# The inverse of each 64-step chunk in an RWKV scan, kept in compressed blocks

## The reference, cut to what matters

```python
def wkv_scan(state0, r, dec, k, v, kk, a, reverse):
    emit = r is not None

    def step(S, inp):
        d_t, k_t, v_t, kk_t, a_t = inp[:5]
        sa = jnp.einsum("bhvk,bhk->bhv", S, -kk_t)
        S = (S * d_t[:, :, None, :] + sa[..., None] * (kk_t * a_t)[:, :, None, :]
             + v_t[..., None] * k_t[:, :, None, :])
        out = jnp.einsum("bhvk,bhk->bhv", S, inp[5]) if emit else None
        return S, out
```

## Time and profile before

| | us |
|---|---|
| median of 3 runs | 2809.04 (2806.54 to 2811.82) |
| profiled execution, its span | 2808.7 |
| scan stage, its first to its last instruction, about | 1073 to 1758 |
| PE busy / DVE / ACT / POOL in the whole span | 2512.4 / 1519.4 / 1099.4 / 735.1 |

### The profile page before, as it was taken

One profiled execution on the slowest core, in us unless ns is written; L12 is line 12 of the kernel. 1 busy time (PEld: TensorE's weight loads), 2 busy tenths in 40 slices (PEclk: granted clock), 3 DMA queues, 4 the chain that ended last, 5 costly groups with the idle time before them and its releaser, 6 DMA issues. The chain is left out here.

```text
span 2808.7 us, 66348 instructions
## 1 busy us (share of the span) xinstructions
PE 2512.4 (89%) x28704; PEld 1935.4 (69%) x28704; DVE 1519.4 (54%) x2491; ACT 1099.4 (39%) x1771; POOL 735.1 (26%) x422
## 2 busy tenths in 40 slices
PE   7998899999889995888888887889999999898997
PEld 5776577777667784777777776768788655475666
DVE  4744589863652213556666663344542466525975
ACT  4633321152453433455545543334422344323133
POOL 2422301422212225555545551100000000032132
PEclk9999999999899996999999999989999999998998
DMA  4224344434335531111111100633522100044431
GB/s 159 83 68 135 128 135 124 122 105 162 116 125 183 201 122 59 43 43 55 38 54 54 32 15 26 240 129 103 159 79 86 57 0 1 11 173 139 137 109 68
DMA packets 90286, 272.63 MB, mean 97 GB/s; under 512 B 13584, under 2 KB 14608, under 8 KB 89872
## 3 DMA queue, kind: packets, MB, share of 16 engines
q1 hardware_dynamic: 73104, 229.25, 25.6%
q10 hardware_dynamic: 16896, 39.16, 4.0%
HBM read 203.01 MB, written 36.70 MB: 85 GB/s over the span
## 5 line engine op out<-in xcount | busy, mean ns | idle before, releaser
L375 PE MATMUL ps<-h_parts_conv,w_parts_one 128*128 128x512 f32 x3168 | 579.8, 343 | 16.9 <-DVE h_parts_conv L361 13.7
L375 PEld LDWEIGHTS ps<-h_parts_conv,w_parts_one 128*128 128x128 f32 x3168 | 492.4, 190 | 107.5 <-issue 24.1
L375 PE MATMUL ps<-scratch_scan 64*64 64x64 f32 (+1 forms) x16704 | 383.1, 234 | 96.2 <-issue 56.1
L375 PEld LDWEIGHTS ps<-scratch_scan 64*64 64x64 f32 x16704 | 345.9, 137 | 139.5 <-issue 105.8
L372 ACT ACTIVATE scratch_scan<-ps 128x384 f32<-128x384 f32 x560 | 238.4, 495 | 331.7 <-PE ps L375 180.3
L443 POOL TENSOR_TENSOR w_parts_one<-ring,w_parts_one 128x1024 fp32r<-128x1024 f32 x83 | 208.2, 2509 | 581.4 <-ACT w_parts_one L372 581.3
L375 PE MATMUL ps<-h_parts_attn,w_parts_rwkv_out 128*128 128x512 f32 (+1 forms) x1536 | 329.2, 373 | 4.6 <-DVE h_parts_attn L369 4.6
L375 PEld LDWEIGHTS ps<-h_parts_attn,w_parts_rwkv_out 128*128 128x128 f32 x1536 | 263.2, 189 | 64.0 <-issue 9.4
L443 POOL TENSOR_TENSOR w_parts_rwkv_out<-ring,w_parts_rwkv_out 128x1024 fp32r<-128x1024 f32 x31 | 74.6, 2409 | 812.5 <-ACT w_parts_rwkv_out L372 812.5
L369 DVE SCALAR_TENSOR_TENSOR scratch_conv<-scratch_conv,vec 128x512 f32<-128x512 f32 (+1 forms) x408 | 252.6, 691 | 0.2
L372 ACT ACTIVATE w_parts_rwkv_out<-ring 128x1024 fp32r<-128x1024 f32 x104 | 109.5, 1056 | 344.0 <-PE ps L375 325.8
(11 more groups left out here) (219 smaller groups left out, 3263.6 us busy)
## 6 DMA issues: line engine op xcount, KB each, us to landing
ring<-in_weights SPq DMA_DIRECT2D x311, 512.0 KB, 3.7
rwkv_spill<-scratch_conv ACTq DMA_DIRECT2D x64, 384.0 KB, 2.3
stream<-rwkv_spill SPq DMA_DIRECT2D x64, 384.0 KB, 3.6
scratch_conv<-scratch_conv SPq DMA_DIRECT2D x120, 103.1 KB, 2.2
scratch_conv<-scratch_conv SPq DMA_DIRECT2D x120, 67.4 KB, 2.0
x_spill<-stream ACTq DMA_DIRECT2D x16, 384.0 KB, 2.5
kept_gate<-scratch_attn ACTq DMA_DIRECT2D x64, 64.0 KB, 2.6
y_spill<-scratch_scan SPq DMA_DIRECT2D x8, 384.0 KB, 2.5
```

What stands on the lines that cost most here:

```text
L375: return nc.tensor.matmul(o, l, r, start=start, stop=stop)
```

## The change

- The inverse is stored compressed. For blocks of b, each row keeps only the b columns of its own block. A level's result is written so that those columns stand repeated over the 64 columns of the chunk (`own`, `half_of`). The full block diagonal form is needed for the transposed P alone, and comes from a mask at the eviction (`own_block`).
- T(n) is 12 matmuls in place of 24. The stationary operand is 64 rows x 128 columns (N of both heads of a pair of chunks), the moving one has 2b columns. Q(n) is 12 as well, with a stationary operand of 128 rows x 64 columns and 2b moving columns. ACT evicts T in two instructions of 64 partitions each, into a tile (`TZ`) of which the other halves stay zero.
- The first doubling becomes a level too (n = 0, b = 1): `first_t` with 6 matmuls of 128 x 128 weights and 4 moving columns, `first_q` with 2, two tiny evictions (`first_t_copy`), and one DVE instruction. `first_inverse`, `p_start` and `p_diagonal` are gone. Levels are now numbered 0 to 5.
- The update is one DVE instruction of 128 x 384 for a level in place of two. Before it ACT writes the part that stays (`other_half`): ten instructions of 128 x 384 for a unit.
- The transposed P of levels 1, 2 and 3 is evicted by DVE with a mask (`turned_inverse`, two instructions each). That of levels 4 and 5 (blocks of 16 and 32) is evicted by ACT, one instruction for each block column with a scale for each row (`turned_blocks`, 8 and 4 instructions). P6, the whole inverse, is evicted by ACT as before.
- The transposed K moves from DVE to ACT.
- POOL masks N in one instruction of 128 x 768 for a level in place of two of 128 x 384. There are six levels for a unit in place of five.

The core of the diff:

```diff
-            def inv_t(w, lv):
...
-                for j in range(HALFC):
-                    for h in range(2):
-                        for par in range(2):
-                            last = mm(bank3(par)[HS[h], j, :], NT[(NLV * w + lv) % 2][HS[par], 2 * j + h, :], PQ[w % 2][HS[par], 2 * j + h, :])
+            def inv_t(w, n):
+                pe.wait_ge(n_masked, masked_at(w, n))
+                inverse_ready(pe, w, n)
+                b = inner(n)
+                for j in range(HALFC):
+                    for par in range(2):
+                        last = mm(PS[:, par * 512 + 2 * b * j:par * 512 + 2 * b * (j + 1)].rearrange("p (x b) -> p x b", x=2),
+                                  NT[n % 2][HS[par], 2 * j:2 * j + 2, :].rearrange("p h t -> p (h t)"), PQ[(n - 1) % 2][HS[par], 2 * j:2 * j + 2, 0:b])
...
+            def inv_q(w, n):
+                pe.wait_ge(t_copied, 2 * product_at(w, n))
+                for e in range(2):
+                    pe.wait_ge(*read_at(f"P{n}", w, e))
+                b = inner(n)
+                t = TZ[:, :, 0:NSTEP * b].rearrange("p x (y j b) -> p y j x b", y=2, b=b)
+                for j in range(HALFC):
+                    for par in range(2):
+                        last = mm(PS[HS[par], 2 * b * j:2 * b * (j + 1)].rearrange("p (x b) -> p x b", x=2), PT[w % 2][:, 2 * j + par, :], t[:, par, j])
+                last.then_inc(q_done, 1)
...
+            def first_t(w):
+                pe.wait_ge(n_masked, masked_at(w, 0))
+                room_for(pe, "T0", w, 0)
+                first = fill_bank("T0", w, 0) * 512
+                o = PS[:, first:first + 2 * NSTEP].rearrange("p (x j y) -> p j y x", x=2, y=2)
+                ones = C("own_half").rearrange("p (y x) -> p y x", y=2)
+                for j in range(HALFC):
+                    last = mm(o[:, j, :, :], NT[0][:, 2 * j:2 * j + 2, :].rearrange("p h t -> p (h t)"), ones)
...
+            def inverse_update(w, n):
...
+                    v.wait_ge(q_done, product_at(w, n))
+                    inverse_ready(v, w, n)
+                    q = PS[:, 0:NSTEP * b].rearrange("p (g b) -> p g b", b=b)
+                    if n < NLV - 1:
+                        v.wait_ge(halved, halved_at(w, n))
+                        vtt(into, into, own(n, q), ALU.add).then_inc(added, 1)
...
+            def turned_inverse(w, n):
+                for e in range(2):
+                    v.wait_ge(*done_at(f"P{n}", w, e))
+                    vtt(blocks(n, PT[w % 2][:, half(e), :]), blocks(n, bank3(fill_bank(f"P{n}", w, e))), own_block(n)).then_inc(*read_inc(f"P{n}", w, e))
...
+            def other_half(w, n):
...
+                    inverse_ready(a, w, n)
+                    before = own(n, PQ[(n - 1) % 2][:, :, 0:inner(n)])
+                    if n < NLV - 1:
+                        act(half_of(n, d), before, ACT.Copy, scale=keep).then_inc(halved, 1)
+                    act(into, before, ACT.Copy, scale=by).then_inc(halved, 1)
...
+            def turned_blocks(w, n):
+                b, first = inner(n), 2 * CH + (8, 12)[n - 4]
+                for e in range(2):
+                    a.wait_ge(*done_at(f"P{n}", w, e))
+                    into, o = PT[w % 2][:, half(e), :], bank3(fill_bank(f"P{n}", w, e))
+                    for k in range(CH // b):
+                        last = act(into[:, :, k * b:k * b + b], o[:, :, k * b:k * b + b], ACT.Copy, scale=C("own_block", first + k, 1))
+                    last.then_inc(*read_inc(f"P{n}", w, e))
```

More of the change, by code:

```diff
@@ L1793, in two_blocks @@
         NT = [take(NSTEP, CH) for _ in range(2)]
-        T1, MT, NE = (take(NSTEP, CH) for _ in range(3))
+        MT, NE = (take(NSTEP, CH) for _ in range(2))
+        TZ, TZ0 = take(2, HALFC * CH), take(2, NSTEP)
         BONV = [take(TT) for _ in range(3)]
@@ new lines, in first_q @@
+            def first_q(w):
+                pe.wait_ge(*read_at("T0", w, 0))
+                room_for(pe, "Q0", w, 0)
+                first = fill_bank("Q0", w, 0) * 512
+                for par in range(2):
+                    o = PS[HS[par], first:first + NSTEP].rearrange("p (j x) -> p x j", x=2)
+                    last = mm(o, C("ident2"), TZ0.rearrange("p x (j y) -> p y x j", y=2)[:, par])
+                last.then_inc(*done_inc("Q0", w, 0))
+            def inv_t(w, n):
+                pe.wait_ge(n_masked, masked_at(w, n))
+                inverse_ready(pe, w, n)
+                b = inner(n)
@@ L2321, in p_start @@
[L2321 to L2329 removed]
+            def inverse_update(w, n):
+                d = w % 2
+                keep = even_rows(n) if d == 0 else odd_rows(n)
+                into, b = half_of(n, d), inner(n)
+                if n == 0:
+                    v.wait_ge(*done_at("Q0", w, 0))
+                    if w > 0:
+                        v.wait_ge(halved, halved_at(w - 1, NLV - 1))
+                    first = fill_bank("Q0", w, 0) * 512
+                    q = PS[:, first:first + NSTEP].rearrange("p (g b) -> p g b", b=1)
+                    vts(into, own(0, q), keep, None, ALU.add).then_inc(*read_inc("Q0", w, 0))
+                else:
+                    v.wait_ge(q_done, product_at(w, n))
[4 more added lines that the diff above has]
+                        vtt(into, into, own(n, q), ALU.add).then_inc(added, 1)
+                    else:
+                        stt(into[:, :, 0], PQ[(n - 1) % 2][:, :, 0:b], keep, q, ALU.mult, ALU.add).then_inc(added, 1)
@@ L2353, in scan_vector @@
                 if two:
-                    inverse_update(w2, 0)
+                    inverse_update(w2, 1)
                 if one:
                     decayed_r(w1)
+                if two:
+                    turned_inverse(w2, 2)
+                if one:
                     decayed_a(w1)
@@ L2419, in scan_scalar, with t_copy, first_t_copy @@
             a.preload_act_table_set(LN_EXP)
-            def t_copy(w, lv, e):
-                a.wait_ge(t_done, level(w, lv, e))
-                act(T1[:, e::2, :], bank3(e), ACT.Copy).then_inc(t_copied, 1)
+            def t_copy(w, n):
+                a.wait_ge(t_done, 2 * product_at(w, n))
+                b = inner(n)
+                t = PS[:, 0:1024].rearrange("p (y z) -> p y z", y=2)[:, :, 0:NSTEP * b].rearrange("p y (j x b) -> p x y j b", x=2, b=b)
+                for h in range(2):
+                    act(TZ[HS[h], h, 0:NSTEP * b].rearrange("p (y j b) -> p y j b", y=2, b=b), t[HS[h], h], ACT.Copy).then_inc(t_copied, 1)
+            def first_t_copy(w):
+                a.wait_ge(*done_at("T0", w, 0))
+                first = fill_bank("T0", w, 0) * 512
+                act(TZ0[HS[0], 0, :], PS[HS[0], first:first + NSTEP], ACT.Copy)
+                act(TZ0[HS[1], 1, :], PS[HS[1], first + NSTEP:first + 2 * NSTEP], ACT.Copy).then_inc(*read_inc("T0", w, 0))
+            def other_half(w, n):
+                d = w % 2
+                by, keep = (odd_rows(n), even_rows(n)) if d == 0 else (even_rows(n), odd_rows(n))
+                into = half_of(n, 1 - d)
+                if n == 0:
+                    if w > 0:
+                        a.wait_ge(added, added_at(w - 1, NLV - 1))
+                    act(into, own(0, by.rearrange("p (g b) -> p g b", b=1).broadcast_to([P, NSTEP, 1])), ACT.Copy).then_inc(halved, 1)
+                else:
+                    inverse_ready(a, w, n)
[3 more added lines that the diff above has]
+                    act(into, before, ACT.Copy, scale=by).then_inc(halved, 1)
             def turned_copy(name, w, e, out):
@@ L2576, in scan_scalar @@
                     a_turned(w2, 1)
+                if one:
+                    other_half(w1, 0)
+                    first_t_copy(w1)
                 if read_pair is not None:
@@ L2580, in scan_scalar @@
                     out_inverse_root(read_pair)
-                turned(5)
-                if one:
-                    p_turned(0, w1, 0)
-                    p_turned(0, w1, 1)
+                if two:
+                    full_turned(w2, 0)
+                    full_turned(w2, 1)
                 if three and w3 % 2 == 0:
```

252 lines of the change are left out of this document (126 added, 126 removed), and 8 rows, old and new, of the table FILLS.

## The result

| | before | after |
|---|---|---|
| median of 4 runs each, same chip | 2809.69 us (2806.54 to 2811.82) | 2894.09 us (2891.30 to 2901.64) |
| ratio | | 1.0304, 95% interval 1.0287 to 1.0320 |
| span of the profiled execution | 2808.7 us | 2890.3 us |

The change makes the kernel 84 us slower. The forecast was 2800 us with a range of 2768 to 2836: the sign was wrong, and the time lies outside.

What follows compares the result with a forecast made beforehand. PE was taken as the engine others wait for, with 13 us of a 39.2 us period lost to instruction fetches and waits. The terms 63 - 48 - 27 + 3 = -9 us gave 2800 us, range 2768 to 2836.

Steps and rivals of the forecast that it cites:

- steps 1 and 2: PE streaming in the scan: 7.8 us a period removed, 11.7 added, so +3.9, or +63 us over 16 periods.
- step 3: PE's instruction fetches: 136 matmuls less a period mean fewer fetches and shorter stops, -48 us, bounds -18 and -74.
- step 4: PE's waits in the scan: shorter for DVE's update (-16), banks freed earlier (-6), smaller ACT copies (-5), sum -27 us.
- step 5: Work added on ACT and DVE: ACT late at b = 16 every second period, +3 us; POOL's masks cost nothing.
- D: Rival: T with 4 moving columns keeps PE too little at work, the granted clock falls: +27, 2827 us, chance 5%.
- C: Rival: on ScalarE's queue `other_half` waits for DVE's last update and delays what follows: +19, 2819 us, chance 12%.
- A: Rival: longer work covers all instruction fetches (-74 for -48), and T covers half the remaining waits (-9): 2765 us, chance 20%.
- B: Rival: T's weight loads are laid bare and PE's stops per fetch stay as long: +35, 2844 us, 15% with a variant.

Runs made afterwards that it cites:

- quad_t: all_parts with T of every level as 24 matmuls on four 64 x 64 quarters of the array in place of 12 on halves: 2803.93 us, ratio 0.9980.
- before_wait: The kernel before with one wait more: PE waits for POOL's first mask of the next unit in front of Q(4): 2856.04 us, ratio 1.0162.
- mask_first: The changed kernel with the first mask of the next unit ahead of `grown_b` on POOL: 2863.75 us, ratio 1.0193.
- all_parts: mask_first with T, Q, `first_t` at 64 moving columns, `first_t_copy` ahead of `other_half`, masked evictions of levels 4 and 5 on DVE: 2832.77 us, ratio 1.0085.
- pad_tq: mask_first with T and Q of levels 1 to 4 and `first_t` widened to 64 moving columns, the added ones unread: 2848.08 us, ratio 1.0134.
- busy: The changed kernel with 13 unread 128x128 matmuls in front of `first_t`'s wait in every second unit: 2885.27 us, ratio 1.0273.

## Why the prediction was wrong

By its own steps:

1. *PE removed, PE added (its steps 1 and 2, +63 us).* The mechanism was right, the size small by a quarter. T was put at 1.34 us, Q at 0.70, `first_t` at 1.3. From their first start to the next instruction they take 1.43 to 1.48, 0.80 to 0.85 and 1.43 us, and `first_q` 0.27. That is 13.0 us in place of 11.7 a turn, +5.2 net, +84 us for 16 turns.
2. *Fewer instructions (its step 3, -48 us).* Right in kind, and larger. The packets of the whole span fell from 230 to 196, where 35 fewer were forecast; PE's idle on issue fell from 57.5 to 4.8 us (1100 to 1830) in place of 20. With the tails this term is near its bound of -74. quad_t shows the cause: as soon as T's slow rows go, 18 us of it return. Streaming and fetches were worked out as two terms, and they are one: longer rows both cost and cover. (The 9.2 fetches of a period are 147 over 16; over the 16.45 periods of that window they are 8.9, which moves the term by less than 1 us.)
3. *Waits for DVE's update (its step 4, -27 us).* PE's transposes wait 0.3 us for it in the steady part in place of 16.7, but its matmuls wait 2.2, and the waits for ACT, which this step wanted smaller, went from 6.7 to 13.7 us. The net of these 525 us is -7. Over the whole scan all of PE's waits for DVE and ACT fall from 44.7 to 31.0 us, -14 in place of -27.
4. *ACT, DVE and POOL (its step 5, +3 us).* This is the step that failed. It said that the first mask is wanted "behind `chain` 9, 4 us after it is made", and cost POOL at nothing "since POOL is idle for 150 us before its masks". A sum of idle time says nothing of when an engine is free. In every second turn POOL's idle time lies ahead of `grown_b`, and the mask behind it. The trace of before had it, in two rows that the prediction did not look at: POOL's masks of the next unit, and PE, which even in the old order came to them 0.80 us early:

```profile
1294.71 1.82 POOL L2624 TENSOR_TENSOR scratch_scan<-scratch_scan 128x768 f32<-128x768 f32 x1
1296.48 8.68 POOL L2602 TENSOR_TENSOR scratch_scan<-scratch_scan,con 128x384 f32<-128x384 f32 x6
```

```profile
1292.91 1.10 PE L375 MATMUL ps<-scratch_scan 64*64 64x64 f32 x56
...
1300.65 3.66 PE L375 MATMUL ps<-scratch_scan 64*64 64x64 f32 x144 [0.80 <-POOL scratch_scan L2602]
```

Chain 9 and Q(4) are in the group at 1292.91. The two halves of the first mask are made from 1296.48 to 1300.6, 2.45 and 1.7 us long; elsewhere two take 1.96 us together, and would end at 1298.4. Moving the first reader from 1300.65 to about 1293.1 thus makes the mask 7.5 us late in this turn and some 5.3 in one with masks of the usual length (an estimate from these rows); before_wait measured 5.50. The prediction allowed for it: "were a mask late by 0.8 us once a period, +13". It is 3.7 us once in two, with the single mask of the change, and with the clock behind it 30 us (mask_first). The other term put at nothing is the clock: the sum has none, and D, which had it, was given 5%.

The rivals were taken as alternatives, with one chance each, and they came together. C (ScalarE's queue) held: `other_half` in front of a copy, though at another place than the T copy. That 17 us were measured where 19 were written is luck: 11 of them are the waits, and the rest is clock, which C did not have. D (the granted clock) held in both of its halves, with a price of about 16 to 21 us for the narrow operands by themselves, at a chance of 5%; the argument against it, "Shorter stops speak against it", missed that the fall needs no stop. A held in its first half, which is why the kernel is not slower still. B, which wanted the stops on issue to stay, did not hold: they went from 57.5 to 4.8 us. In all: 30 us for the late mask, 16 for the narrow operands, 17 for the copy, 2 for the evictions, 65 by single steps and 61 for all together (2894.09 to 2832.77). What is left in all_parts, 23 us over the kernel before, is where the sum said -9. Its trace has 21 of them: 10 in the scan, 7 ahead of it and 4 behind. In the scan T and Q were 21 us too cheap, the waits for DVE and ACT 16 us too low (they fall from 44.7 to 33.4 us there), and the fetches gave back some 20 us more than was written, which makes +8 of the 10. The 11 us outside the scan stay open.

## What to carry to other kernels

When an edit moves a wait forward on the critical engine, look up when the awaited instruction runs in the trace, and what stands before it in its own queue, in each kind of turn; an engine's total of idle time does not answer that. Rivals that can all be true at once are terms of the sum and not alternatives, and several small losses of one sign belong in the range together. A narrower moving operand gained nothing here, where a row costs what its weights cost, and it lost clock; the same compressed blocks with T on four quarters and wider operands (quad_t) are faster than the kernel before.

## What the runs showed of the hardware

- The granted clock fell to 0.50 with PE never idle for longer than 0.19 us in the nine us before, when the matmuls had few moving columns (mask_first, 1285.3, and likewise before 1244.4, 1367.2 and 1449.2); with 64 columns and the same weight loads it stayed at 1.00 over the same code (pad_tq, 1175 to 1340). Stops of 2.67 us (pad_tq), 3.70 (changed kernel) and 5.50 us (before_wait) stand beside a fall too. The Trainium skill, "TensorE: Matmul & The Clock Gate", section "HAM oscillation — how this bites in real kernels", tells of the fall behind an idle gap; the traces agree on that, and show the other one beside it.
- Weights of 64 x 128 on alternating halves take 1.43 to 1.48 us for 24 rows whether 4 or 64 columns move, counted to the next instruction's start; drawn with the tail they are 1.55 us with 64 columns (all_parts), where weights of 64 x 64 on four quarters are drawn with 0.90 us for 48 rows (quad_t).
- 13 matmuls that compute nothing, put where PE stopped in every second turn, did not make a kernel slower but some 5 us faster in its 15 turns (busy, 645.1 against 650.3; medians 2885.27 and 2894.09).
- A stream with slower and fewer rows (11623 in 525 us in all_parts, against 15367 before) hides the fetches of instructions almost whole: 2.6 us of idle on issue in 525 us, against 20.7 with T in quarters and 52.2 in the kernel before.
